# Eight of 24 gate panels as seven block products, between the RWKV tiles of a two-layer trunk kernel

## The reference

```python
    merged = jnp.zeros_like(x)
    for i, y_i in enumerate((y_a, y_b, y_c, y_d)):
        merged = merged + jax.nn.sigmoid(u @ P['w_gate'][l, i]) * (y_i @ P['w_branch'][l, i])
    x = x + g2 * (merged @ P['w_out'][l])
```

## Time and profile before

| | us |
|---|---|
| median of 3 runs | 3064.17 (3063.32 to 3065.41) |
| the profiled execution, its own time | 3064.26 |
| its span, first to last instruction | 3062.6 |
| PE busy | 3028.3 (99%) |
| DVE busy | 1385.5 (45%) |
| ACT busy | 408.5 (13%) |
| POOL busy | 1370.4 (45%) |

### The profile page before, as it was taken

One profiled execution on the slowest core, in us unless ns is written; L12 is line 12 of the kernel. 1 busy time (PEld: TensorE's weight loads), 2 busy tenths in 40 slices (PEclk: granted clock), 3 DMA queues, 4 the chain that ended last, 5 costly groups with the idle time before them and its releaser, 6 DMA issues.

```text
span 3062.6 us, 48411 instructions
## 1 busy us (share of the span) xinstructions
PE 3028.3 (99%) x19694; PEld 2488.2 (81%) x19694; DVE 1385.5 (45%) x3045; ACT 408.5 (13%) x766; POOL 1370.4 (45%) x1453
## 2 busy tenths in 40 slices
PE   8999999999999999999999999999999999999999
PEld 5889888677777878898878898876777778789987
DVE  4446522454233464556244564324533344555642
ACT  2000002302111120000010000022021111200000
POOL 4879530210000339896368894311100013499943
PEclk9999999999999999999999999999999999999999
DMA  6543223541111334222246322334411114122222
GB/s 261 216 162 117 95 103 127 177 128 41 53 53 60 106 122 163 104 83 90 77 176 223 124 83 86 137 117 143 131 55 53 53 60 158 69 83 83 83 86 68
DMA packets 73534, 337.81 MB, mean 110 GB/s; under 512 B 10592, under 2 KB 27744, under 8 KB 40288
## 3 DMA queue, kind: packets, MB, share of 16 engines
q1 hardware_dynamic: 63936, 312.03, 28.7%
q0 software_dynamic: 6816, 18.88, 2.1%
q10 hardware_dynamic: 2560, 3.80, 0.4%
HBM read 326.55 MB, written 6.02 MB: 109 GB/s over the span
## 4 chain that ended last, share of the span: by engine, by line
PE 93%; POOL 3%; DVE 2%; ACT 1%; issue 1%; DMA 0%; SPq 0%; POOLq 0%; DVEq 0%; ACTq 0%
PE ps L915 92%; DVE ws L2097 1%; DMA ws<-w_ada 0%; DVE u L2097 0%; ACT u L1801 0%; POOL masked_room L846 0%; ACT ws L1801 0%; DVE y L2097 0%; POOL ws L805 0%; PE ps L1625 0%; POOL ws L811 0%; POOL ws L809 0%; DVE proj L2097 0%; POOL ws L813 0%; POOL ws L808 0%
## 5 line engine op out<-in xcount | busy, mean ns | idle before, releaser
L915 PE MATMUL ps<-u,ring 128*128 128x272 f32 (+1 forms) x5088 | 1203.3, 387 | 6.5 <-ACT u L1801 2.2
L2097 DVE TENSOR_TENSOR ws<-ws,ps 128x136 f32<-128x136 f32 (+4 forms) x1658 | 623.3, 401 | 1163.3 <-PE ps L915 1138.0
L915 PEld LDWEIGHTS ps<-u,ring 128*128 128x128 f32 x5088 | 917.9, 190 | 210.8 <-issue 24.4
L791 POOL TENSOR_TENSOR masked_room<-ring 128x512 f32<-128x512 f32 (+1 forms) x36 | 46.8, 1299 | 897.7 <-DVE pause L2868 620.6
L915 PE MATMUL ps<-y,ws 128*128 128x272 f32 (+1 forms) x1616 | 343.5, 348 | 0.0
L915 PEld LDWEIGHTS ps<-y,ws 128*128 128x128 f32 x1616 | 265.8, 190 | 36.2 <-DVE ws L2097 3.7
L915 PE MATMUL ps<-y,ring 128*128 128x272 f32 (+1 forms) x1376 | 278.8, 340 | 2.0 <-POOL ws L813 2.0
L1801 ACT ACTIVATE ws<-ws 128x272 f32<-128x272 f32 (+5 forms) x210 | 130.2, 638 | 1095.2 <-DVE ws L2097 1043.7
L1801 ACT ACTIVATE ws<-ps 128x272 f32<-128x272 f32 (+2 forms) x318 | 122.3, 395 | 965.9 <-PE ps L915 965.9
L915 PEld LDWEIGHTS ps<-y,ring 128*128 128x128 f32 x1376 | 220.0, 190 | 31.9 <-POOL ws L813 2.8
L915 PE MATMUL ps<-proj,ring 128*128 128x272 f32 x832 | 200.4, 393 | 1.4 <-DVE proj L2097 1.4
(11 more groups left out here) (232 smaller groups left out, 3340.8 us busy)
## 6 DMA issues: line engine op xcount, KB each, us to landing
ring<-w_up SPq DMA_DIRECT2D x88, 1024.0 KB, 5.0
proj<-w_ada SPq DMA_DIRECT2D x45, 1024.0 KB, 6.9
ring<-w_down SPq DMA_DIRECT2D x32, 1024.0 KB, 4.9
ring<-w_gate SPq DMA_DIRECT2D x32, 1024.0 KB, 5.0
ws<-w_ada SPq DMA_DIRECT2D x26, 1024.0 KB, 4.9
ring<-w_in SPq DMA_DIRECT2D x22, 1024.0 KB, 4.9
ws<-cache SPq DMA_DIRECT2D x128, 128.0 KB, 3.1
ws<-cache POOLq DMA_DIRECT2D x128, 128.0 KB, 3.4
```

What stands on the lines that cost most here:

```text
L791: nc.gpsimd.tensor_tensor(sums[:, 0], a21, a22, ALU.add).then_inc(w_sums.sem, 1)
L915: return nc.tensor.matmul(out, lhsT, rhs, start=start, stop=stop, skip_group_check=skip)
L2097: return V.tensor_tensor(out, a, b, op)
```

## The change

Pairs g = 2 to 9 of each layer (`SPLIT = (2, 10)`, the 32 units that stood in the tiles) are worked off as seven products of 2x2 blocks: blocks of 512 inputs by 128 outputs of the weights, and of 512 inputs by 272 tokens of `u`. `split_fill(g, n)` has parts n = 0 to 7, and `piece(k)` of tile tt is now part k % 8 of pair 2 + 2tt + k // 8. Parts 0 to 6 are a product of four matmuls each, parts 3 and 5 have half a branch unit (two matmuls) behind it, part 7 is two branch halves. So a pair is 28 gate and 8 branch matmuls.

- POOL makes five token sums once a layer (`split_token_sums`), after the pooling products, and four weight sums for each pair (`split_weight_sums`) once both of its panels are loaded. S1, S2 and S4 go to the columns 512 to 2047 of the branch panel's ring slot, which the 512 columns of that panel leave free, and S3 over a block of the gate panel.
- ACT copies the first product out of bank 4 (`first`), then takes four sigmoids, three of them of sums that DVE makes in SBUF.
- DVE adds the products from banks 6 and 7 (`U2`, `U3`, `c22`, `c21`, `c12`) and multiplies the gates with the branch halves in bank 5 or 6 (`m11`, `m22`, `m21`, `m12`, with an addition into `merged` from g = 4 on).
- Units 0 to 7 and 40 to 47 stay, with other numbers in their signals (`plain_fill`).

```diff
+                def split_token_sums():
+                    b11, b12, b21, b22 = u[:, 0:4, 0:HALF], u[:, 0:4, HALF:T], u[:, 4:8, 0:HALF], u[:, 4:8, HALF:T]
+                    pool.wait_ge(pool_pe.sem, pool_pe.upto(l, 1))
+                    nc.gpsimd.tensor_tensor(split_t12[:, 0], b12, b11, ALU.subtract).then_inc(sp_sums.sem, 1)
+                    pool.wait_ge(sp_sums.sem, sp_sums.upto(l, 1))
+                    nc.gpsimd.tensor_tensor(split_t12[:, 1], b22, split_t12[:, 0], ALU.subtract).then_inc(sp_sums.sem, 1)
+                    pool.wait_ge(sp_sums.sem, sp_sums.upto(l, 2))
+                    nc.gpsimd.tensor_tensor(split_t4a, b21[:, 0:3], split_t12[:, 1, 0:3], ALU.subtract).then_inc(sp_sums.sem, 1)
+                    nc.gpsimd.tensor_tensor(split_t4b, b21[:, 3], split_t12[:, 1, 3], ALU.subtract).then_inc(sp_sums.sem, 1)
+                    pool.wait_ge(rp_pe.sem, rp_pe.upto(l, 2))
+                    pool.wait_ge(rp_dve.sem, rp_dve.upto(l, 1))
+                    nc.gpsimd.tensor_tensor(split_t3, b22, b12, ALU.subtract).then_inc(sp_sums.sem, 1)
+
+                def split_weight_sums(g):
+                    s = panel_wait(pool, l, "gate", 2 * g)
+                    panel_wait(pool, l, "gate", 2 * g + 1)
+                    w = ring[:, s, :].rearrange("p (k m) -> p k m", k=KT)
+                    a11, a12, a21, a22 = w[:, 0:4, 0:P], w[:, 4:8, 0:P], w[:, 0:4, P:256], w[:, 4:8, P:256]
+                    s1, s2, s3, s4 = split_sums(l, g)
+                    done = 4 * (g - SPLIT[0])
+                    nc.gpsimd.tensor_tensor(s1, a21, a22, ALU.add).then_inc(sp_weights.sem, 1)
+                    pool.wait_ge(sp_weights.sem, sp_weights.upto(l, done + 1))
+                    nc.gpsimd.tensor_tensor(s2, s1, a11, ALU.subtract).then_inc(sp_weights.sem, 1)
+                    nc.gpsimd.tensor_tensor(s3, a11, a21, ALU.subtract).then_inc(sp_weights.sem, 1)
+                    pool.wait_ge(sp_weights.sem, sp_weights.upto(l, done + 2))
+                    nc.gpsimd.tensor_tensor(s4, a12, s2, ALU.subtract).then_inc(sp_weights.sem, 1)
+
                 weight_sums(0)
...
                 cache_loads(4, 32)
+                split_token_sums()
+                for g in range(*SPLIT):
+                    split_weight_sums(g)
                 pool.wait_ge(gn_dve.sem, gn_dve.upto(l, 1))
                 for p in range(4):
                     block_sums("gate_b", 2 * p, unit_of("gate_b", p), 4)
+                    def product(bank, w, v, start):
+                        for k in range(4):
+                            m = mm(ps[:, bank, 0:HALF], w(k), v(k), start=start and k == 0, stop=k == 3, skip=True)
+                        m.then_inc(part.sem, 1)
+
+                    def branch_half(bank, c, hf):
+                        for k in range(2):
+                            m = mm(ps[:, bank, 0:HALF], ring[:, branch, k * 256 + c * P:k * 256 + c * P + P],
+                                   y[:, BRANCH_ROWS[g // 4] + k, hf * HALF:hf * HALF + HALF], start=k == 0, stop=k == 1)
+                        return m
+
+                    if n == 0:
+                        panel(l, "gate", 2 * g)
+                        if first:
+                            pe_.wait_ge(fill_gate.sem, fill_gate.upto(l, 4 * SPLIT[0]))
+                        else:
+                            split_act(pe_, l, g - 1, "g11")
+                        product(4, raw(0, 0), tok(0, 0), True)
+                    elif n == 1:
+                        pe_.wait_ge(sp_weights.sem, sp_weights.upto(l, ready + 2))
+                        pe_.wait_ge(sp_sums.sem, sp_sums.upto(l, 2))
+                        if not first:
+                            split_dve(pe_, l, g - 1, "m21")
+                        product(6, weights(s2), sums(1), True)
+                    elif n == 2:
+                        split_act(pe_, l, g, "first")
+                        product(4, raw(4, 0), tok(4, 0), False)
+                    elif n == 3:
+                        pe_.wait_ge(sp_weights.sem, sp_weights.upto(l, ready + 3))
+                        pe_.wait_ge(sp_sums.sem, sp_sums.upto(l, 5))
+                        split_dve(pe_, l, g, "U2")
+                        product(6, weights(s3), sums(2), False)
+                        panel(l, "gate", 2 * g + 1)
+                        if first:
+                            pe_.wait_ge(fill_sum.sem, fill_sum.upto(l, 4 * SPLIT[0]))
+                        else:
+                            split_dve(pe_, l, g - 1, "m12")
+                        branch_half(5, 0, 0).then_inc(sp_branch.sem, 1)
+                    elif n == 4:
+                        if not first:
+                            split_dve(pe_, l, g - 1, "c12")
+                        product(7, weights(s1), sums(0), True)
+                    elif n == 5:
+                        split_dve(pe_, l, g, "U3")
+                        product(6, raw(4, P), sums(3), False)
+                        split_dve(pe_, l, g, "m11")
+                        branch_half(5, 1, 1).then_inc(sp_branch.sem, 1)
+                    elif n == 6:
+                        pe_.wait_ge(sp_weights.sem, sp_weights.upto(l, ready + 4))
+                        split_dve(pe_, l, g, "c22")
+                        product(7, weights(s4), tok(4, HALF), False)
+                    else:
+                        split_dve(pe_, l, g, "c21")
+                        branch_half(6, 1, 0).then_inc(sp_branch.sem, 1)
+                        split_dve(pe_, l, g, "m22")
+                        branch_half(5, 0, 1).then_inc(part.sem, 1)
 
                 def scores(h):
                     ft, po = h // 2, HD * (h % 2)
...
@@ -1608,7 +1773,7 @@
                 for tt in range(NTT):
                     def piece(k):
 
-                        fill(8 * tt + 8 + k // 2, 5 * (k % 2), 5 * (k % 2) + 5)
+                        split_fill(SPLIT[0] + 2 * tt + k // 8, k % 8)
 
+            def split_merge(l, g, v, bank, c, hf):
+
+                dst = merged[:, (2 * g + c) % KT, hf * HALF:hf * HALF + HALF]
+                ins = tt_(v if g >= 4 else dst, v, ps[:, bank, 0:HALF], MUL)
+                if g >= 4:
+                    link(l, ins)
+                    ins = tt_(dst, dst, v, ADD)
+                ins.then_inc(sp_dve.sem, 1)
+
...
+            def split_last_merges(l, g):
+                split_act(dve, l, g, "g21")
+                split_branch(dve, l, g, "B10")
+                split_merge(l, g, split_first, 6, 1, 0)
+                split_act(dve, l, g, "g12")
+                split_part(dve, l, g, 8)
+                split_merge(l, g, split_second, 5, 0, 1)
 
             def merges(l, a, b):
                 for n in range(a, b):
...
-                        fill_merge(l, 8 * tt + 7)
+                        split_sum_12(l, g0 - 1)
                     tile_pe(1)
                     masked(MA, 0, M16U)
                     masked(MB, 1, M16L)
                     tt_(ME1, ps[:, 0:2, 2 * P + CH:3 * P], across(cst[:, M16U:M16U + CH], 2), MUL)
                     masked(ET32, 1, E32L)
                     masked(E64, 1, E64L).then_inc(rw_dve.sem, 1)
+                    if tt:
+                        split_last_merges(l, g0 - 1)
                     dve.wait_ge(rw_dve.sem, rw_dve.upto(l, 2 + tt * RW_DVE))
                     tt_(ME, MA, across(cst[:, ID64:ID64 + CH], NH), ADD)
...
                     added(MF, ME)
                     masked(LakT, 2, SU64).then_inc(rw_dve.sem, 1)
-                    merge(0)
+                    split_second_sum(l, g0)
...
                     added(ME, MF).then_inc(rw_dve.sem, 1)
-                    merge(2)
+                    split_sum_21(l, g0)
+                    split_merge_22(l, g0)
...
+                    split_last_merges(l, g0)
                     for ch in range(2):
                         tt_(stmp[:, :, :], sbd[:, :, :], over(pend[:, :, ch], P), MUL)
                         if ch == 1:
-                            merge(5)
+                            split_third_sum(l, g0 + 1)
...
                         m.then_inc(rw_dve.sem, 1)
                         dve.wait_ge(rw_dve.sem, rw_dve.upto(l, 10 + 2 * ch + tt * RW_DVE))
-                    merge(6)
+                    split_sum_21(l, g0 + 1)
+                    split_merge_22(l, g0 + 1)
                     tile_pe(17)
```

More of the change, by code:

```diff
@@ L133, with plain_fill @@
 FILLS = 48
+SPLIT = (2, 10)
+PLAIN_FILLS = FILLS - 4 * (SPLIT[1] - SPLIT[0])
+SPLIT_PE = {"B00": 1, "B11": 2, "B10": 3}
+SPLIT_ACT = {n: i + 1 for i, n in enumerate(("first", "g11", "g22", "g21", "g12"))}
+SPLIT_DVE = {n: i + 1 for i, n in enumerate(("U2", "U3", "m11", "c22", "c21", "m22", "c12", "m21", "m12"))}
+def plain_fill(f):
+    return f if f < 4 * SPLIT[0] else f - 4 * (SPLIT[1] - SPLIT[0])
 ADA_FIRST, ADA_UP = 8, 28
@@ L1408, in fills, with split_fill, raw, tok @@
                         fill(n)
+                def split_fill(g, n):
```

(69 more changed lines are left out.)

86 lines of the change are left out of this document (75 added, 11 removed).

## The result

| | us, median (range) | runs | ratio to before, 95% interval |
|---|---|---|---|
| before, on the chip of the result | 3064.34 (3063.32 to 3065.41) | 6 | |
| the changed kernel | 3046.47 (3044.85 to 3048.82) | 6 | 0.9941 [0.9931, 0.9951] |

The forecast was 3044 us, 3035 to 3054. The change is faster by 0.6%, as forecast.

What follows compares the result with a forecast made beforehand. PE's own work was taken as the bound, busy 3028.3 of 3062.6 us. 3064.26 - 29.4 (removed products) + 3.0 (step A) + 6.4 (step C) = 3044.3, so 3044 us, range 3035 to 3054.

Steps and rivals of the forecast that it cites:

- Removed work: Gate products in the tiles: 64 matmuls, 128 instructions fewer at 0.23 us each, 29.4 us less PE work.
- Step A: Where two tiles meet: PE waits about 0.5 us for DVE at three places a layer, +3.0 us, bounds 0 and 6.
- Step C: Starts of tiles 2 and 3: POOL's sums block DVE, delaying the MC copy; 4 x 1.6 = +6.4 us, bounds 0 and 10.8.
- The clock: Behind the tiles: a fall from 2.4 to 1.2 GHz costs about 1.8 us; one to three new ones only in a rival.
- stalls at more places: Rival: both lock bounds at tile starts plus some mid-tile stalls, or one to three new clock falls: 3053 us, chance 0.13.
- the second burst in each tile: POOL's sums after piece 7, covered by two pieces and two steps: 0, at worst 8 times 1 us.
- the token sums before the tiles: POOL's sums near merge 4, 0.55 us of slack to PE's branch half: taken as 0, bounds 0 and 1.4 us.
- ACT's copy: Inside a tile: one ACT copy more for a pair, costed at nothing, covered by the pieces.
- DVE's additions in mid-tile: Inside a tile: DVE gets five sums for a pair, costed at nothing since most steps keep about 1 us of cover.
- Full cover: Rival: POOL lands in a gap of DVE and step A is not late: 3034.9 us, 3037.9 with step A's 3; chance 0.20.
- POOL gives no turns: Rival: DVE stays out for all four POOL operations, 4.0 us at four places: 3054 us, within the second rival's chance.
- The slower case: Rival: each of 14 POOL bursts inside the tiles holds up a step by 2.7 us: 3075.7 us, chance 0.03.

Runs made afterwards that it cites:

- drop_four: The kernel before, with one of eight gate matmuls left out in units 8 to 39 (64 fewer), POOL and DVE unchanged: 3034.76 us, 0.9907.
- hold_pool: The changed kernel, with POOL's weight sums of odd pairs held until DVE's MC copy for step C is done: 3036.40 us, 0.991.
- hold_and_behind: hold_pool, with DVE's two last merges of a pair also put behind the additions ME and ME1: 3036.32 us, 0.9911.
- y_on_act: hold_pool, with each tile's output copy moved from DVE's list to ACT's: 3034.76 us, 0.9904.
- pool_halves: The changed kernel, with each of POOL's weight sums written as two operations of half the width: 3038.01 us, 0.9914.
- ctrl: The changed kernel again with no edit, as control: 3046.31 us, 0.9944.

## Why the prediction was right, point by point

As in the prediction, A is the start of step A and E the end of piece 15.

- **Removed work.** 29.4 us expected; drop_four measured 29.5 between profiled executions. The tile window of 47.2 us and the 19566 instructions came as said. That PE was the bound was the point on which the sign hung.
- **Step A, mis-sized.** The step "there are 3 such places a layer: +3.0 us". The wait was 0.41 us (0.46 forecast) but in tiles 2 and 3 only, 1.6 us in all. Pair 3, whose merges stand at the end of tile 0, has no additions, so DVE is 0.4 us shorter there; I used that for step C and forgot it here.
- **Step C, the right mechanism.** 1.6 us at four places, 6.4, was forecast; it was 1.21, 2.23 and 1.98 at three, 5.4 us. The bursts there began at A + 3.9, 3.6 and 3.4, at the early end of the forecast's A + 3.5 to 4.5. In tile 2 of layer 1 the panel landed late, POOL began at A + 5.1, later than forecast and behind ME1, and there was no wait. The forecast's 2.7 us for A + 3.5 was too long in two places: it took 0.7 us of slack where hold_pool shows 1.0, and turns of 1.26 + 0.38 = 1.64 us where POOL's operations start 1.31 to 1.40 us apart. That POOL would start so early rests on a step that the prediction didn't say, that the branch panel lands 0.6 us or more behind the gate panel although the gate load now goes out 0.92 us earlier. It did: in tile 3 of layer 0 the branch panel took 3.9 us from its issue, where the earlier trace rows have 4.7 and 5.7. hold_pool and hold_and_behind show that POOL made every wait of this kind.
- **The clock, the term that failed.** The sum cost it at nothing and left it to the rival "stalls at more places" at 1.8 us a fall. That price holds, but two falls more, 3.5 us, came with my own main case. The errors in steps A and C, 2.4 us too much together, hid most of it: 3044.3 against 3045.21. That the number came out so near is luck. The clock's part is also larger in the median, 3046.47, than in the profiled execution: two of the six executions have a mean granted clock of 0.997, the profiled one 0.998.
- **Costed at nothing, rightly:** the second burst in each tile, the token sums before the tiles, ACT's copy, DVE's additions in mid-tile. None of them shows in PE's waits.
- **A sign that was off.** POOL's groups were to start 4 to 5 us after each step A, while the prediction's own count had A + 3.5 to 4.5. At the starts of tiles 1 to 3 they start 3.4 to 5.1 us after it, in tile 0 of layer 0 6.3.
- **The rivals.** Full cover did not come by itself; y_on_act makes it come, and it gives 3034.76, where the rival had 3034.9. "POOL gives no turns" is refuted by the profile after, where three DVE operations in a row each lost one turn, and by pool_halves. The slower case would have needed 1.9 us at each of 14 bursts; three had a cost.

What stays open: why the clock fell in the sample part, 0, 1 or 2 times in a profile, without a wait. The place is always the row of 64x8 products, once in each layer, but no run was made on that. Nor does any profile show the executions of ctrl and of hold_pool whose times are the medians, so the two falls by which hold_pool gains more than its 6.0 us of waits are read from the times and mean clocks only.

## What to carry to other kernels

When work moves to GpSimd, list what VectorE does in those microseconds with two SBUF inputs, and charge each such operation up to one GpSimd operation if the next product hangs on it. The remedies are cheap: let GpSimd wait until the urgent VectorE operation is done (-9.9 us here, of which 6.0 are the waits themselves), or cut its operations in half (-8.3 us, of which 4.4 are waits). A wait of some 2 us in an otherwise full TensorE is to be charged with more than its length, since the clock may fall with it.
